# Two decoder layers' attention: the values of two jobs in a row and the scores of two more behind them, every other step

## The chip, the cores and the metric

The kernel runs on one core of one Trainium2 chip. The metric is device time in microseconds (us), of one launch from start to end. A profiled execution of the same program gives, for every instruction, its engine, start and duration. The engines are TensorE (PE for its matmuls, PEld for its weight loads), VectorE (DVE), ScalarE (ACT), GpSimd (POOL) and SyncE (SP, which issues the weights' DMAs).

## The reference, cut to what matters

The whole program is a block with a sparse-attention mixer, a cross attention and a feed-forward part, and behind it two equal layers. The change touches the attention of these two layers (16 query heads of width 64, two groups of keys and values, a band of 128 positions, so 256 keys for each block of 128 queries, and an extra sink in each softmax):

```python
def sliding_window_attention(q, k, v, sinks):      # T = 512, BLOCK = 128, 16 heads, 2 KV heads
    ...
    s = jnp.einsum('bnqkgd,bnskd->bnkgqs', qb, kb) * scale      # 128 queries x 256 keys
    s = jnp.where(mask, s, -jnp.inf)
    m = jnp.maximum(jnp.max(s, axis=-1, keepdims=True), sink)
    p = jnp.exp(s - m)
    p = p / (jnp.sum(p, axis=-1, keepdims=True) + jnp.exp(sink - m))
    o = jnp.einsum('bnkgqs,bnskd->bnqkgd', p, vb)
    ...
for l in range(2):
    ...
    a_out = sliding_window_attention(q, k, v, sinks[l])
    c_out = conformer_conv(u, ug, ...)             # 31 taps, layer norm, silu, a product
    merged = jax.nn.sigmoid(ga) * a_out + jax.nn.sigmoid(gb) * c_out
    x = x + merged @ w_out[l]
    x = x + ffn(rmsnorm(x))
```

## The kernel before

Activations lie feature-major in SBUF (128 features of a tile by 512 positions). Weights stream through three slots; each is split by ACT and DVE into a high and a low part, so a product is three matmuls of 512 columns (`products`, L415 to L417). PSUM is one tile `bank` of eight banks.

Of each layer, `layer_pe`, `layer_act`, `layer_dve` and a loop on POOL write out the order of each engine by hand. The attention of a layer is `LJ` = 32 jobs (4 query blocks by 8 pairs of heads; jobs 24 to 31 belong to the first block and have 128 keys, not 256). A loop over steps t = 0 to 35 runs through all of them, on all engines alike. In step t of the kernel before:

- PE: `scores(t)` (L2110; two heads at once on 64 rows of the array each, into banks 2 and 3 for an even job, 0 and 1 for an odd one; it waits until the softmax has read the job two before it), then `turn(t-3)` (L2120, transposes of the probabilities into bank 4; it waits for ACT's `scaled` of the job and for ACT's copy of the job turned before), then some chunks of other products (`fill_chunks`; one chunk is three matmuls of 512 columns, how many come in which step is the table `FILL_AT`), then `values(t-4)` (L2133; two heads side by side on 64 columns of the array each, into bank 6; it waits for ACT's copy of the job). In step 1 `rotate(8)` (L2028, the rotary part of the last query tile) comes between the scores and the chunks; in step 3 the sum over channels for the layer norm (L2170) is last, in step 7 its sum of squares (L333).
- ACT: `copy_turned(t-3)` (L2275, bank 4 to SBUF; it waits for PE's turn), `exps(t)` (L2260), `scaled(t-1)` (L2267, the probabilities times one over their sum), then other work of that step: tanh of a gate tile (L2293), half of a weight unit's high part (L785, L788), squares (L2299), silu (L2306) and so on.
- DVE: `softmax(t, t-1)` (L2425, mask and row maximum of job t; L2429, reciprocal of job t-1), `gated(t-4)` (L2437, the attention's result from bank 6 into the gate tile; it waits for PE's values), then evictions of finished fill tiles (L2471), halves of low parts (L793, L797), centring (L2486), taps of the convolution (L2355) in steps 0 and 1.

Every engine takes its own list strictly in this order, so whatever stands behind a waiting instruction waits as well.

Of the kernel before, what the change touches and what calls it, by code (L numbers as in the profile page):

```python
# [100 lines left out]
def build(nc, w, x, mem, pos, pack, tables, cmask, w2, wg, rope2, out):  # L101
    ctx = ExitStack()
    with ctx:
# [1742 lines left out]
        def cross_dve(dve):  # L1846
# [76 lines left out]
            for j in range(11):  # L1923
# [29 lines left out]
        FILL_FIRST = 5  # L1953
        FILL_AT = {1: 6, 2: 2, 3: 1, 5: 4, 6: 4, 7: 2, 9: 3, 10: 2, 12: 3, 14: 6, 15: 5, 16: 3, 17: 4, 18: 4, 19: 2,
                   20: 3, 21: 2, 22: 1, 23: 2, 24: 2, 25: 2, 26: 1, 27: 2, 28: 2, 29: 3, 30: 3, 31: 1}
# [11 lines left out]
        OUT_AT = {32: (0,), 33: (1,), 34: (2,), 35: (3,)}  # L1967
        STEPS = LJ + LAG_V

        def prob_at(j):  # L1970
# [27 lines left out]
        def layer_pe(pe, L):  # L1998
# [124 lines left out]
            def values(j):  # L2123
                i, g = block_of(j), j % 8 // 4
                first = 1 if i == 0 else 0
                pe.wait_ge(A["turned_copied"], L * LJ + j + 1)
                if j == 0:
                    pe.wait_ge(q_rope, L * 9 + 9)
                else:
                    pe.wait_ge(A["gated"], L * LJ + j)  # L2130
                for c in range(first, 2):
                    for e in range(2):
                        mm = pe.matmul(bank[HD * e:HD * e + HD, 6, 0:P], lv[:, i - 1 + c, g * HD:(g + 1) * HD],  # L2133
                                       lprobT[:, j % 2, 2 * e + c, :], start=(c == first), stop=(c == 1))
                mm.then_inc(A["pv"], 1)
# [11 lines left out]
            for t in range(STEPS):  # L2147
                if t < LJ:
                    scores(t)
                if t == 1:  # L2150
# [8 lines left out]
                if t in OUT_AT:  # L2159
# [3 lines left out]
                    out_products(((1, 1), (0, 0), (0, 1)), OUT_AT[t])  # L2163
                if 0 <= t - LAG_V < LJ:
                    values(t - LAG_V)
                if t == AT_SUM:
# [167 lines left out]
        def layer_dve(dve, L):  # L2334
# [96 lines left out]
            def gated(j):  # L2431
                i, tile = block_of(j), j % 8
                dst = sga[:, tile, i * P:(i + 1) * P]
                dve.wait_ge(A["pv"], L * LJ + j + 1)
                if j == 0:
                    dve.wait_ge(l_g, L * 16 + 8)
                dve.scalar_tensor_tensor(out=dst, in0=dst, scalar=1.0, in1=bank[:, 6, 0:P], op0=ALU.add, op1=ALU.mult).then_inc(A["gated"], 1)  # L2437

# [15 lines left out]
            for t in range(STEPS):  # L2454
                softmax(t, t - 1)
                if 0 <= t - LAG_V < LJ:
                    gated(t - LAG_V)
                if t == STEPS - 1:
# [292 lines left out]
```

## Time and profile before

| | us |
|---|---|
| median of 3 runs | 2248.47 |
| lowest, highest | 2247.74, 2249.46 |
| the profiled execution, its whole time | 2249.38 |
| the profiled execution, span of its instructions | 2247.4 |
| PE busy | 2225.3 (99%) |
| DVE busy | 1241.2 (55%) |
| ACT busy | 929.0 (41%) |
| POOL busy | 217.5 (10%) |

The chain of work that ended last is PE for 88% of the span, DVE for 7%, ACT for 2%. The 36 steps of the first layer lie from 1033.4 to about 1155 us of the span, those of the second from 1725.9 to about 1848. How to read it: a PE that is busy is not PE at its peak, since the ends of matmuls are modelled and overlap; the distance from the start of one group to the start of the next says more than the durations.

### The profile page before, as it was taken

To read this page: it belongs to the slowest core of one execution; us is meant where nothing else is said; L and a number is where in the kernel's file an instruction comes from. 1 tells how busy PE (TensorE), PEld (TensorE's weight loads), DVE (VectorE), ACT (ScalarE), POOL (GpSimd) and SP (SyncE) were. 2 spreads that over 40 slices of the span, in tenths; PEclk is the share of its full clock that TensorE was granted. 3 is DMA by queue.
4 is the path that set the end of the run, shared out by engine and by line. 5 is a ranking of instruction groups with operands and counts; after the bars stand their busy time and mean duration, and the time that the engine had idled before them with its cause. 6 is when DMAs were issued, how large, how long until landed. Compare 5 with 4: busy or idle time off the path is not lost.

```text
span 2247.4 us, 29309 instructions
## 1 busy us (share of the span) xinstructions
PE 2225.3 (99%) x11388; PEld 1822.5 (81%) x11388; DVE 1241.2 (55%) x1836; ACT 929.0 (41%) x1491; POOL 217.5 (10%) x209
## 2 busy tenths in 40 slices
PE   9999999999999999999999999999999999999999
PEld 7887888898888888886678888888887668888887
DVE  6467656445444225999664444333889664544422
ACT  5545454354333225235954333222323973433321
POOL 3000032011000001012031000001003122000000
PEclk9999999999999999999999999999999999999999
DMA  6221033122222231321122322222221112322222
GB/s 221 102 76 57 20 122 124 55 73 98 104 100 93 94 113 69 113 75 57 55 78 78 110 93 93 99 107 105 105 83 57 38 66 85 113 100 105 94 99 88
DMA packets 30484, 203.19 MB, mean 90 GB/s; under 512 B 3504, under 2 KB 4144, under 8 KB 6704
## 3 DMA queue, kind: packets, MB, share of 16 engines
q1 hardware_dynamic: 29088, 197.34, 24.4%
q10 hardware_dynamic: 1296, 4.46, 0.5%
q8 instruction: 69, 1.13, 0.2%
q14 instruction: 31, 0.25, 0.0%
HBM read 199.69 MB, written 2.10 MB: 90 GB/s over the span
## 4 chain that ended last, share of the span: by engine, by line
PE 88%; DVE 7%; ACT 2%; issue 2%; POOL 1%; DMA 0%; ACTq 0%; DVEq 0%; POOLq 0%
PE bank L415 25%; PE bank L417 25%; PE bank L416 25%; DVE cy L2355 3%; PE bank L2133 1%; PE bank L1002 1%; PE bank L2120 1%; PE bank L2110 1%; DVE w_lo L301 1%; PE bank L973 1%; POOL acc L324 1%; PE bank L990 1%; PE bank L2010 1%; PE bank L1593 1%; PE bank L1570 1%
## 5 line engine op out<-in xcount | busy, mean ns | idle before, releaser
L415 PE MATMUL bank<-x_hi,w_hi 128*128 128x512 f32 (+1 forms) x2032 | 790.1, 389 | 6.1 <-DVE x_lo L1766 2.3
L417 PE MATMUL bank<-x_hi,w_lo 128*128 128x512 f32 (+1 forms) x2032 | 775.0, 381 | 0.0
L416 PE MATMUL bank<-x_lo,w_hi 128*128 128x512 f32 (+1 forms) x2032 | 774.0, 381 | 0.0
L301 DVE TENSOR_TENSOR w_lo<-w_raw,w_hi 128x2048 fp32r<-128x2048 f32 x167 | 386.2, 2313 | 412.4 <-ACT w_hi L297 412.4
L297 ACT ACTIVATE w_hi<-w_raw 128x2048 fp32r<-128x2048 f32 x167 | 319.7, 1916 | 585.1 <-PE bank L417 583.2
L415 PEld LDWEIGHTS bank<-x_hi,w_hi 128*128 128x128 f32 x2032 | 382.2, 188 | 83.8 <-issue 6.8
L417 PEld LDWEIGHTS bank<-x_hi,w_lo 128*128 128x128 f32 x2032 | 381.9, 188 | 75.0
L416 PEld LDWEIGHTS bank<-x_lo,w_hi 128*128 128x128 f32 x2032 | 382.5, 188 | 72.5 <-issue 2.9
L415 PE MATMUL bank<-f_hi,w_hi 128*128 128x512 f32 (+1 forms) x572 | 213.3, 373 | 0.0
L416 PE MATMUL bank<-f_lo,w_hi 128*128 128x512 f32 (+1 forms) x572 | 213.2, 373 | 0.0
L417 PE MATMUL bank<-f_hi,w_lo 128*128 128x512 f32 (+1 forms) x572 | 213.2, 373 | 0.0
L2355 DVE SCALAR_TENSOR_TENSOR cy<-la,gains,cy 128x512 f32<-128x512 f32 x240 | 172.8, 790 | 0.0
L563 DVE TENSOR_TENSOR bank<-bank,rbc 128x512 f32<-128x512 f32 x66 | 46.0, 697 | 166.9 <-PE bank L417 158.8
L416 PEld LDWEIGHTS bank<-f_lo,w_hi 128*128 128x128 f32 x572 | 107.7, 188 | 19.1
L415 PEld LDWEIGHTS bank<-f_hi,w_hi 128*128 128x128 f32 x572 | 107.7, 188 | 18.8
L417 PEld LDWEIGHTS bank<-f_hi,w_lo 128*128 128x128 f32 x572 | 107.7, 188 | 18.8
L324 POOL TENSOR_TENSOR acc<-acc,sq 128x512 f32<-128x512 f32 (+1 forms) x48 | 77.7, 1618 | 144.2 <-ACT sq L308 140.5
L552 ACT ACTIVATE f_hi<-bank 128x512 f32 x66 | 39.6, 600 | 116.3 <-DVE bank L569 116.3
L571 DVE TENSOR_TENSOR f_lo<-bank,f_hi 128x512 f32 x66 | 45.7, 692 | 59.3 <-ACT f_hi L552 59.3
L2260 ACT ACTIVATE lprob<-lprob,small 128x257 f32<-128x257 f32 (+1 forms) x128 | 60.4, 475 | 25.4 <-DVE small L2425 25.1
L2425 DVE CUSTOM_DVE_ANT_0 lprob<-bank,mask_b,neg_sink 128x256 f32<-128x256 f32 (+1 forms) x128 | 60.0, 506 | 6.1 <-PE bank L2110 6.1
L550 ACT ACTIVATE silu<-bank 128x512 f32<-128x512 f32 x66 | 38.9, 589 | 54.7 <-DVE bank L563 54.5
(355 smaller groups left out, 2598.3 us busy)
## 6 DMA issues: line engine op xcount, KB each, us to landing
w_raw<-w_d SPq DMA_DIRECT2D x184, 1024.0 KB, 4.8
out_d<-h SPq DMA_DIRECT2D x8, 256.0 KB, 6.4
h<-x_d ACTq DMA_DIRECT2D x3, 512.0 KB, 9.4
tab<-rope_d ACTq DMA_DIRECT2D x2, 640.0 KB, 3.9
memT<-mem_d ACTq DMA_DIRECT2D x1, 1024.0 KB, 4.8
w_raw<-w_d SPq DMA_DIRECT2D x2, 256.0 KB, 4.0
h<-x_d ACTq DMA_DIRECT2D x2, 256.0 KB, 5.8
w_raw<-w_d SPq DMA_DIRECT2D x1, 512.0 KB, 6.8
```

Of the source, the lines that this page charges most:

```text
L297: act.activation(w_hi[:, u.slot, :], w_raw[:, u.slot, :], ACT.Copy).then_inc(hi_ready, 1)
L301: dve.tensor_tensor(w_lo[:, u.slot, :], w_raw[:, u.slot, :], w_hi[:, u.slot, :], ALU.subtract).then_inc(lo_ready, 1)
L324: pool.tensor_tensor(acc[:, 0:width], sq[:, 0, 0:width] if k == 1 else acc[:, 0:width], sq[:, k % 2, 0:width], ALU.add).then_inc(acc_ready, 1)
L415: pe.matmul(dst, wh[:, k, cols], hi[:, kx_, at:at + width], start=start, stop=False)
L416: pe.matmul(dst, wh[:, k, cols], lo[:, kx_, at:at + width], start=False, stop=False)
L417: return pe.matmul(dst, wl[:, k, cols], hi[:, kx_, at:at + width], start=False, stop=stop)
L552: act.activation(pick(f_hi, j, i), up, ACT.Copy).then_inc(f_hi_done, 1)
L563: dve.tensor_tensor(g, g, rbc[:, :], ALU.mult).then_inc(gu_scaled, 1)
L571: dve.tensor_tensor(pick(f_lo, j, i), up, pick(f_hi, j, i), ALU.subtract).then_inc(f_lo_done, 1)
L2260: act.activation(row, row, ACT.Exp, bias=asm(j, 0, e), scale=-1.0, accum_out=asm(j, 4, e)).then_inc(A["exp"], 1)
L2355: dve.scalar_tensor_tensor(out=cy[:, m, :], in0=src, scalar=wt, in1=cy[:, m, :], op0=ALU.mult, op1=ALU.add).then_inc(l_tap, 1)
L2425: dve.tensor_tensor_reduce(lprob[:, prob_at(j), e, c0:2 * P], bank[:, score_bank(j) + e, c0:2 * P], mask_b[:, c0:2 * P], query_factor(j, e ...
```

## The change

Two functions name the jobs of a step. `scores_at(t)`: job 0 in step 0, jobs t and t+1 in an odd step, none in an even one. `values_at(t)`: jobs t-4 and t-3 in an even step, none in an odd one. So the scores of every even job come one step earlier, and the values of every odd job one step earlier, in the very step in which it is turned. The two jobs of a pair write their values side by side in bank 6 (columns 0 to 127 and 128 to 255). DVE's `gated` of both jobs stands in the even step and waits for the values of both. One chunk moves from step 3 to step 4 and one from step 7 to step 8. Instructions, their number and their operands are otherwise the same.

```diff
-        FILL_AT = {1: 6, 2: 2, 3: 1, 5: 4, 6: 4, 7: 2, 9: 3, 10: 2, 12: 3, ...
+        FILL_AT = {1: 6, 2: 2, 4: 1, 5: 4, 6: 4, 7: 1, 8: 1, 9: 3, 10: 2, 12: 3, ...
...
+        def scores_at(t):
+            return [j for j in ((0,) if t == 0 else (t, t + 1) if t % 2 else ()) if j < LJ]
+        def values_at(t):
+            return [] if t % 2 or t < LAG_V else [t - LAG_V, t - LAG_V + 1]
...
             def values(j):
                 pe.wait_ge(A["turned_copied"], L * LJ + j + 1)
...
-                else:
+                elif j % 2 == 0:
                     pe.wait_ge(A["gated"], L * LJ + j)
...
-                        mm = pe.matmul(bank[HD * e:HD * e + HD, 6, 0:P], lv[...], lprobT[...], ...)
+                        mm = pe.matmul(bank[HD * e:HD * e + HD, 6, j % 2 * P:(j % 2 + 1) * P], lv[...], lprobT[...], ...)
...
             for t in range(STEPS):
-                if t < LJ:
-                    scores(t)
+                for j in scores_at(t):
+                    scores(j)
...
-                if 0 <= t - LAG_V < LJ:
-                    values(t - LAG_V)
+                for j in values_at(t):
+                    values(j)
...
             def gated(j):
-                dve.wait_ge(A["pv"], L * LJ + j + 1)
+                dve.wait_ge(A["pv"], L * LJ + j // 2 * 2 + 2)
...
                 softmax(t, t - 1)
-                if 0 <= t - LAG_V < LJ:
-                    gated(t - LAG_V)
+                for j in values_at(t):
+                    gated(j)
```

On PE, steps 0 and 1 of the first layer, before (L2110 scores, of jobs 0 and 1 here and of job 2 at the end; L2028 `rotate(8)`; L415 the first matmul of a chunk; 17 further rows of the six chunks are left out ahead of the last two):

```order
L2110 MATMUL bank<-lq_121 128x256
L2110 MATMUL bank<-lkx_122,lq_121 128x256
L2110 MATMUL bank<-lq_121 128x256
L2110 MATMUL bank<-lkx_122,lq_121 128x256
L2028 MATMUL bank<-lq_121,perm_q_134 128x512
L415 MATMUL bank<-x_hi_69,w_hi_65 128x512
...
L2110 MATMUL bank<-lq_121 128x256
L2110 MATMUL bank<-lkx_122,lq_121 128x256
```

The same place after (L2118 is the scores' line now, L2036 the rotation's):

```order
L2118 MATMUL bank<-lq_121 128x256
L2118 MATMUL bank<-lkx_122,lq_121 128x256
L2118 MATMUL bank<-lq_121 128x256
L2118 MATMUL bank<-lkx_122,lq_121 128x256
L2118 MATMUL bank<-lq_121 128x256
L2118 MATMUL bank<-lkx_122,lq_121 128x256
L2036 MATMUL bank<-lq_121,perm_q_134 128x512
L415 MATMUL bank<-x_hi_69,w_hi_65 128x512
```

The scores of job 2 have moved ahead of the rotation and of the six chunks of step 1.

On PE, step 4 and the start of step 5, before (scores of job 4, turn of job 1, values of job 0, scores of job 5, turn of job 2, chunks):

```order
L2110 MATMUL bank<-lkx_122,lq_121 128x256
L2110 MATMUL bank<-lq_121 128x256
L2120 MATMUL bank<-ident_50,lprob_138 128x128 x4
L2133 MATMUL bank<-lprobT_139,lv_123 64x128 x4
L2110 MATMUL bank<-lkx_122,lq_121 128x256
L2110 MATMUL bank<-lq_121 128x256
L2120 MATMUL bank<-ident_50,lprob_138 128x128 x4
L415 MATMUL bank<-x_hi_69,w_hi_65 128x512
```

The same place after (turn of job 1, a chunk, values of jobs 0 and 1, scores of jobs 5 and 6, turn of job 2):

```order
L2128 MATMUL bank<-ident_50,lprob_138 128x128 x4
L415 MATMUL bank<-x_hi_69,w_hi_65 128x512
L416 MATMUL bank<-x_lo_70,w_hi_65 128x512
L417 MATMUL bank<-x_hi_69,w_lo_66 128x512
L2141 MATMUL bank<-lprobT_139,lv_123 64x128 x8
L2118 MATMUL bank<-lkx_122,lq_121 128x256
L2118 MATMUL bank<-lq_121 128x256
L2118 MATMUL bank<-lkx_122,lq_121 128x256
L2118 MATMUL bank<-lq_121 128x256
L2128 MATMUL bank<-ident_50,lprob_138 128x128 x4
```

The values of job 1 now stand between the turn of job 1 and the scores of jobs 5 and 6, with one chunk and the values of job 0 between them and the turn; before, they stood in step 5, behind four chunks.

On DVE, the end of step 4, before (L2429 reciprocal, L2437 `gated(0)`, L793 half of a low part, L2486 centring, L2425 the softmax of step 5):

```order
L2429 RECIPROCAL small_62<-small_62 128x2
L2437 SCALAR_TENSOR_TENSOR sga_128<-sga_128,bank 128x128
L793 TENSOR_TENSOR w_lo_66<-w_raw_64,w_hi_65 128x1024
L2486 TENSOR_TENSOR cy_125<-cy_125,acc_72 128x512 x2
L2425 ISA lprob_138,small_62<-bank,mask_b_53,neg_sink_61,rcol_head_60 128x256
```

After (`gated` is L2445, of jobs 0 and 1):

```order
L2437 RECIPROCAL small_62<-small_62 128x2
L2445 SCALAR_TENSOR_TENSOR sga_128<-sga_128,bank 128x128 x2
L793 TENSOR_TENSOR w_lo_66<-w_raw_64,w_hi_65 128x1024
L2495 TENSOR_TENSOR cy_125<-cy_125,acc_72 128x512 x2
L2433 ISA lprob_138,small_62<-bank,mask_b_53,neg_sink_61,rcol_head_60 128x256
```

The split, the centring and the softmax of step 5 stand behind a `gated` that needs the values of job 1 too.

## Rows read from the trace of the kernel before

**Rows 1.** Page, busy time of the engines: share of the span, instructions.

```profile
PE 2225.3 (99%) x11388; PEld 1822.5 (81%) x11388; DVE 1241.2 (55%) x1836; ACT 929.0 (41%) x1491; POOL 217.5 (10%) x209
```

**Rows 2.** Windows: us, busy (instructions) of PE PEld DVE ACT POOL, granted clock, DMA, GB/s.

```profile
1046.00:1100.00 54.00, 52.15 (x340) 36.50 (x338) 34.61 (x110) 52.50 (x127) 8.04 (x18) 1.00 0.11 40
1100.00:1155.00 55.00, 54.38 (x354) 37.39 (x352) 35.31 (x110) 43.00 (x124) 13.56 (x18) 1.00 0.17 58
```

**Rows 3.** Timeline of PE, the turns that waited for ACT's copy: idle before in brackets.

```profile
1050.98 0.63 PE L2120 MATMUL bank<-ident,lprob 128*128 128x128 f32 x4 [1.03 <-ACT lprobT L2275]
...
1070.86 0.63 PE L2120 MATMUL bank<-ident,lprob 128*128 128x128 f32 x4 [0.82 <-ACT lprobT L2275]
```

**Rows 4.** Timeline of PE, step 11 (no chunks): start, us, line, tiles, array, form.

```profile
1073.40 0.48 PE L2110 MATMUL bank<-lq 64*128 64x256 f32 x1
1074.04 0.65 PE L2120 MATMUL bank<-ident,lprob 128*128 128x128 f32 x4
1074.62 0.66 PE L2133 MATMUL bank<-lprobT,lv 128*64 128x128 f32 x8
1075.21 0.48 PE L2110 MATMUL bank<-lkx,lq 64*128 64x256 f32 x1
```

**Rows 5.** Timeline of PE, steps 0 to 4.

```profile
1033.66 0.38 PE L2110 MATMUL bank<-lq 64*128 64x256 f32 x1
1033.88 0.38 PE L2110 MATMUL bank<-lq 64*128 64x256 f32 x1
1034.09 0.38 PE L2110 MATMUL bank<-lq 64*128 64x256 f32 x1
1034.44 1.12 PE L2028 MATMUL bank<-lq,perm_q 128*128 128x512 f32 x2
...
1039.60 0.48 PE L2110 MATMUL bank<-lq 64*128 64x256 f32 x1
1040.23 0.50 PE L415 MATMUL bank<-x_hi,w_hi 128*128 128x512 f32 x1
...
1041.81 0.48 PE L2110 MATMUL bank<-lq 64*128 64x256 f32 x1
1043.92 3.60 PE L2170 MATMUL bank<-cy,ones 128*128 128x512 f32 x8
1047.44 0.48 PE L2110 MATMUL bank<-lkx,lq 64*128 64x256 f32 x1
```

**Rows 6.** Timeline of DVE, softmax of job 0, then step 4.

```profile
1037.69 0.53 DVE L2425 CUSTOM_DVE_ANT_0 lprob<-bank,mask_b,neg_sink 128x256 f32<-128x256 f32 x1
1038.16 0.07 DVE L2425 DVE_READ_ACCUMULATOR2_ANT small<- 128x1 f32 x1
...
1050.68 1.93 DVE L793 TENSOR_TENSOR w_lo<-w_raw,w_hi 128x1024 fp32r<-128x1024 f32 x1
1052.53 1.28 DVE L2486 TENSOR_TENSOR cy<-cy,acc 128x512 f32<-128x512 f32 x2
```

**Rows 7.** Timeline of ACT, step 4 to the copy of step 5's start.

```profile
1050.26 0.58 ACT L2275 ACTIVATE lprobT<-bank 128x512 f32<-128x512 f32 x1
1050.73 0.50 ACT L2260 ACTIVATE lprob<-lprob,small 128x257 f32<-128x257 f32 x1
1051.72 0.90 ACT L2267 ACTIVATE lprob<-lprob,small 128x256 f32<-128x256 f32 x2
...
1054.51 0.58 ACT L2275 ACTIVATE lprobT<-bank 128x512 f32<-128x512 f32 x1
```

**Rows 8.** The values' line: count, duration ns min/median/max, first and last start, forms.

```profile
L2133 PE MATMUL bank<-lprobT,lv x448: 272/273/324, 1048.7 to 1847.7; 128*64 128x128 f32 x150
```

**Rows 9.** Windows, the one place where the granted clock falls.

```profile
220.88:224.29 3.41, 2.78 (x20) 2.02 (x19) 3.06 (x6) 2.57 (x7) 1.27 (x1) 1.00 0.40 171
224.29:227.70 3.41, 3.41 (x19) 3.17 (x17) 2.10 (x5) 1.27 (x4) 0.00 (x0) 0.50 0.01 2
```

**Rows 10.** Timeline of PE, just before the clock falls.

```profile
222.40 1.05 PE L333 MATMUL bank<-ones,z 128*128 128x1 f32 x8 [0.63 <-POOL z L2577]
```

More of the change, by code:

```diff
@@ L1953, in build @@
         FILL_FIRST = 5
-        FILL_AT = {1: 6, 2: 2, 3: 1, 5: 4, 6: 4, 7: 2, 9: 3, 10: 2, 12: 3, 14: 6, 15: 5, 16: 3, 17: 4, 18: 4, 19: 2,
+        FILL_AT = {1: 6, 2: 2, 4: 1, 5: 4, 6: 4, 7: 1, 8: 1, 9: 3, 10: 2, 12: 3, 14: 6, 15: 5, 16: 3, 17: 4, 18: 4, 19: 2,
                    20: 3, 21: 2, 22: 1, 23: 2, 24: 2, 25: 2, 26: 1, 27: 2, 28: 2, 29: 3, 30: 3, 31: 1}
@@ L2132, in values @@
                     for e in range(2):
-                        mm = pe.matmul(bank[HD * e:HD * e + HD, 6, 0:P], lv[:, i - 1 + c, g * HD:(g + 1) * HD],
+                        mm = pe.matmul(bank[HD * e:HD * e + HD, 6, j % 2 * P:(j % 2 + 1) * P], lv[:, i - 1 + c, g * HD:(g + 1) * HD],
                                        lprobT[:, j % 2, 2 * e + c, :], start=(c == first), stop=(c == 1))
@@ L2433, in gated @@
                 dst = sga[:, tile, i * P:(i + 1) * P]
-                dve.wait_ge(A["pv"], L * LJ + j + 1)
+                dve.wait_ge(A["pv"], L * LJ + j // 2 * 2 + 2)
                 if j == 0:
                     dve.wait_ge(l_g, L * 16 + 8)
-                dve.scalar_tensor_tensor(out=dst, in0=dst, scalar=1.0, in1=bank[:, 6, 0:P], op0=ALU.add, op1=ALU.mult).then_inc(A["gated"], 1)
+                dve.scalar_tensor_tensor(out=dst, in0=dst, scalar=1.0, in1=bank[:, 6, j % 2 * P:(j % 2 + 1) * P],
+                                         op0=ALU.add, op1=ALU.mult).then_inc(A["gated"], 1)
             def conv_gated(k):
```

## The prediction, made before the changed kernel ran

> **What bounds the kernel now.** First the page's busy line [rows 1]: PE is busy 99% of the span, ACT 41%, DVE 55%. So PE bounds the whole, and a gap or a slow stretch of PE goes into the time one for one. Then the windows of the first layer's attention [rows 2], where the shares are others: from 1046 to 1100 us (steps 3 to 16) ACT is busy 52.50 of 54 us, and from 1100 to 1155 (the rest) 43.00 of 55. In the first stretch ACT has 1.5 us of slack in all, so a faster PE can bring no more than that there, and an ACT that starts later stays late. PE's turns show the same thing: at 1050.98 and 1070.86 they had waited 1.03 and 0.82 us for ACT's copy of the job before [rows 3]. Only in the second stretch is PE alone the bound. Last, the timelines, read from start to start: they give what one group of PE's instructions costs (step 11) [rows 4], how the loop starts [rows 5], and what DVE and ACT do beside it [rows 6, 7].
>
> **What is gained: the joints.** A step without chunks is 1.81 us: scores 1073.40 to 1074.04 (0.64), turn to 1074.62 (0.58), values to 1075.21 (0.59) [rows 4]. Each of the three uses the array in another shape (64 rows, all of it, 64 columns), and part of each cost is the joint. How much, jobs in a row tell. At the start of the loop jobs 0 and 1 are scored without anything between: starts at 1033.66, 1033.88 and 1034.09, 0.215 apart, two of these to a job [rows 5]. A second job of scores thus costs 0.43, not 0.64: 0.21 saved. The eight instructions of a job's values span 0.66 us, [rows 4], of which the last takes 0.27, the line's median [rows 8], so their starts lie within 0.39, three intervals between four pairs of heads' halves, the first of them longer; a second job adds four of the short ones, about 0.11 each, 0.44 in place of 0.59: 0.15 saved. The turn of an odd step now runs into chunks or the next turn and not into values: 0.14, from the same kind of difference (0.58 for four transposes that need 0.11 each). Sum 0.50 for two steps. With 16 pairs that is 8 us a layer, 16 us in both, if PE bounded everywhere.
>
> The Trainium skill has a reason for it: "TensorEngine Tiling (Array Packing)", section Key Properties, says that a change of tiling mode, and not just of tile, drains the array. By that alone the change is a gain everywhere; its time is the first rival below.
>
> **What is lost at the start.** The scores of job 2 stand in step 1 now. Their bank is free when DVE has read job 0, and DVE does that only behind three taps: its read ends at 1038.16 + 0.07 = 1038.23 [rows 6]. PE is done with job 1 at about 1034.3 and goes on with the rotation at 1034.44 [rows 5]. In the new order it stands still from 1034.3 to 1038.3, 4 us, with rotation and six chunks queued behind. Followed on: scores of job 2 and a joint, 0.5, so the rotation starts at 1038.85, not 1034.44. Rotation and six chunks take 1039.60 - 1034.44 = 5.2, until 1044.0. Two chunks of step 2, 1.4 (1041.81 - 1040.23 is 1.58 with joints [rows 5]), then at 1045.45 two jobs of scores (1.07) and the turn of job 0 (0.45, no chunk behind it now), then the channel sum, 3.43 (1047.44 less the joint less 1043.92). It ends at 1050.4, and before it ended at 1047.35: 3.0 us late. What comes after it hangs on it: DVE's mean and centring, ACT's squares (which ended at 1050.26, when the copy of job 1 starts [rows 7]) and so that copy, now at 1053.3. That is 3.0 us on an ACT that has no slack to give back. The two edits of the table (one chunk from step 3 to 4, from 7 to 8) cost nothing by themselves: the chunk was done in step 3 ahead of the sum, and is done in step 4 ahead of the values of job 0, and no one waits for the tile that it belongs to until step 5 or 8.
>
> **What is lost in the loop.** Values of the odd job now wait for ACT's copy in the same step, and the next scores and the next turn are queued behind them. From the start of an odd job's copy to the start of the next copy PE needs: copy and signal 0.72 (1050.26 to the turn that it frees at 1050.98 [rows 3, 7]), values 0.44, joint 0.1, two jobs of scores 0.96, joint 0.1, turn 0.49, signal 0.2; 3.0 us. ACT has copy, two exponentials and two scalings to do meanwhile, 0.47 + 0.99 + 0.80 = 2.3 us [rows 7]. Before, that turn waited for the copy alone, 0.72 + 0.49 + 0.2 = 1.4, and ACT was never short of work. Where ACT is the late one and has nothing else in the step, it now idles about 0.7. In step 4 DVE adds to it: `gated` of both jobs waits for the values of job 1 (1054.0 + 0.6), and the split (1.1), the centring (1.28 for two) and the softmax of job 5 come after; so the second pair of squares ends near 1058.1 and the copy of job 2 starts there, not at 1054.51 [rows 6, 7]: 3.5 us late by then. In steps 6 to 16 I count two idle spots of 0.7 (steps 10 and 12, which have no other work on ACT) and part of a third: 5.0 us late at step 16.
>
> **What comes back.** From step 17 on PE bounds. Nine pairs at 0.50 are 4.5 us. Against it stand steps with few chunks (20, 22, 26, 28), in which the copy of the odd job is not ready when PE comes to its values; with ACT busy 43 of 55 us [rows 2], and many of its copies queued behind halves of weights, I take three waits of 0.7, 2.1 us in all. Net 2.4 back. A layer is thus 5.0 - 2.4 = 2.6 us slower, both layers 5.2.
>
> **The clock.** The new standstill of 4 us is longer than any in this trace's loops (1.03 [rows 3]). The granted clock falls once in the trace, to 0.50, the 1.2 GHz level, from 224.29 to 227.70 [rows 9]; before it PE had stood idle 0.63 us and then done eight matmuls of one column [rows 10], far less of a pause than 4 us. So I expect the fall in each layer, in or right behind the standstill. Its price by that row: it lasts 3.4 us, in which half the work is done, 1.7 us at most; part of it will lie in the standstill, where it costs nothing. Bounds 0 and 3.4 (if it takes a second such stretch to come back); I take 1.2 a layer, 2.4 in both. It delays the same chain as above, so it is added in full.
>
> The Trainium skill says so too: "TensorE: Matmul & The Clock Gate", section Why this matters for your kernels, warns that an idle gap between bursts of matmuls throws the clock back to half. Without that the sum is 5.2, with it 7.6.
>
> **The sum.** The profiled execution took 2249.38 with a span of 2247.4; it is 0.9 above the median 2248.47. The differences are the same for both: 2249.38 + 7.6 = 2257.0 for such an execution, and 2248.47 + 7.6 = 2256.0 for the median. 0.2% of it is 4.5 us, about what a measurement of this kernel can tell from no change.
>
> **The rivals.**
> - *The joints win (faster).* PE is 99% busy, and the gain of 0.50 a pair is exact arithmetic of the trace. If ACT and DVE just shift with PE and only the standstill is lost, it is 16 - 8 = 8 us less: 2240.5. Against it: ACT's 52.50 of 54 us. Chance 0.10.
> - *The standstill is swallowed (same).* PE waited 1.03 and 0.82 later anyway; if the chain behind the sum has more play than I read, what is left is the loss in the loop against what comes back, -1 to +1 a layer: 2246.5 to 2250.5, take 2249. Chance 0.14.
> - *The clock stays up.* Everything else as forecast: 2253.7. Chance 0.22.
> - *Worse.* The clock needs two stretches to come back, or the waits for copies stop PE at each of the late pairs and nothing comes back: 3 to 5 us a layer more than 2.6 to 3.8, 2261 to 2266. Chance 0.08. It decides if PE's granted clock is 0.50 for 6.8 us behind the standstill.
> - The forecast: 2256.0, with 2252.5 to 2260 as its own range. Chance 0.46.
>
> That the change doesn't do what it says is not a case: the order of PE shows the pairs at both places. The range takes the forecast, the clock that stays up and most of the swallowed standstill: 2247.5 to 2261. Slower by over 0.2%: the forecast, the worse case and two thirds of the clock case, 0.46 + 0.08 + 0.15 = 0.69, rounded to 0.70. Same: 0.07 of the clock case and nearly all of the swallowed one, 0.19. Faster 0.11.
>
> **What the profile after would show.** PE idle for 4 us ahead of the third pair of scores in each layer, released by DVE's softmax of job 0. The granted clock at 0.50 for about 3.4 us there. The channel sum of step 3 ending 3 us later against the loop's start. New waits of PE's values for ACT's copy in steps 4 and 8 and in some of the late steps, and fewer idle spots where PE's weights waited at a joint. A start to start of 0.43 for the second job of scores and 0.44 for the second of values. The forecast is wrong if ACT reaches step 16 less than 3 us late, if the late half brings more than 4 us back, or if the clock stays at 1.00.

## The result and the profile after

The changed kernel takes 2261.86 us (median of five runs, 2260.77 to 2263.60), the kernel before 2249.22 in the six runs beside it: 1.0057 of it, with an interval of 1.0047 to 1.0068, so 12.6 us slower. A sixth run of the changed kernel was in a slow state, 3156.38 us at a mean granted clock of 0.651, and with it the median is 2262.39, from which the expectations below reckon. The profiled execution took 2261.18 us with a span of 2259.2. The forecast was slower by 7.6, 2256.0, with a range to 2261: the sign came true, the size did not, and the time lies 0.9 outside the range.

The page's busy line, which answers to [rows 1]:

```profile
PE 2217.4 (98%) x11388; PEld 1826.4 (81%) x11388; DVE 1242.8 (55%) x1836; ACT 928.6 (41%) x1491; POOL 212.6 (9%) x209
```

PE is busy 7.9 us less and the span is 11.8 longer: it lost time by waiting (work at half clock counts as busy in full, so this line does not show what the clock took). The view of PE's waits (who waited for what; us in total, times, the longest) names the places. In the kernel before only the turns waited for copies, 4.8 us in all; the other lines are new:

```profile
PE bank L2141 <- ACT lprobT L2283: 10.1, 10, 1.5
PE bank L2118 <- DVE small L2433: 7.7, 2, 3.9
PE bank L2128 <- ACT lprobT L2283: 3.5, 8, 0.8
PE bank L415 <- DVE sgb L2454: 3.0, 2, 1.5
```

These are values waiting for the copy (L2141), the scores of job 2 (L2118), turns (L2128), and the first output product behind the attention (L415).

**The start.** PE's timeline, which answers to [rows 5], and the windows around it (us, then busy time and instructions of PE, PEld, DVE, ACT, POOL, the granted clock, DMA share, GB/s), which answer to [rows 9]:

```profile
1037.38 0.76 PE L2118 MATMUL bank<-lq 64*128 64x256 f32 x1 [3.87 <-DVE small L2433]
1037.94 0.63 PE L2118 MATMUL bank<-lq 64*128 64x256 f32 x1
1038.54 2.08 PE L2036 MATMUL bank<-lq,perm_q 128*128 128x512 f32 x2
```

```profile
1032.40:1035.33 2.93, 1.11 (x8) 0.71 (x8) 2.90 (x5) 0.00 (x0) 2.28 (x4) 1.00 0.00 0
1035.33:1042.16 6.83, 4.78 (x11) 2.74 (x12) 4.90 (x14) 2.99 (x10) 0.36 (x1) 0.50 0.00 0
1042.16:1046.00 3.84, 3.84 (x18) 3.18 (x17) 2.50 (x6) 0.00 (x0) 0.00 (x0) 1.00 0.00 0
...
1735.06:1741.89 6.83, 5.76 (x13) 3.52 (x14) 3.92 (x12) 2.99 (x10) 0.00 (x0) 0.50 0.00 1
```

PE stands still for 3.87 us, as forecast, and the clock falls to 1.2 GHz within that. But it stays there for 6.83 us, twice as long as in the trace before, and 4.78 of them are work at half speed. The second layer shows the same (3.88 us idle until 1736.13, clock 0.50 from 1735.06 to 1741.89), but there only 1.07 of the 6.83 us lie in the standstill, and 5.76 are work.

**The loop.** The odd job's values behind a wait for its copy, in steps 4, 8, 16 and 22, and in step 12 a turn:

```profile
1055.21 0.66 PE L2141 MATMUL bank<-lprobT,lv 128*64 128x128 f32 x8 [1.54 <-ACT lprobT L2283]
1070.75 0.66 PE L2141 MATMUL bank<-lprobT,lv 128*64 128x128 f32 x8 [1.33 <-ACT lprobT L2283]
1081.27 0.63 PE L2128 MATMUL bank<-ident,lprob 128*128 128x128 f32 x4 [0.78 <-ACT lprobT L2283]
1102.41 0.66 PE L2141 MATMUL bank<-lprobT,lv 128*64 128x128 f32 x8 [1.04 <-ACT lprobT L2283]
1123.80 0.44 PE L2141 MATMUL bank<-lprobT,lv 128*64 128x128 f32 x4 [0.78 <-ACT lprobT L2283]
```

What DVE and ACT do behind the first of them (`gated` of both jobs, the split, the centring; then ACT's copy of job 2), against [rows 6, 7]:

```profile
1055.91 0.49 DVE L2445 SCALAR_TENSOR_TENSOR sga<-sga,bank 128x128 f32<-128x128 f32 x2 [0.90 <-PE bank L2141]
1056.32 1.22 DVE L793 TENSOR_TENSOR w_lo<-w_raw,w_hi 128x1024 fp32r<-128x1024 f32 x1
1057.45 1.29 DVE L2495 TENSOR_TENSOR cy<-cy,acc 128x512 f32<-128x512 f32 x2
```

```profile
1059.31 0.58 ACT L2283 ACTIVATE lprobT<-bank 128x512 f32<-128x512 f32 x1
```

The first window of [rows 2] shows that ACT, busy 52.50 of 54 us before, now has holes, 48.96 of 54. PE sinks from 52.15 to 49.56:

```profile
1046.00:1100.00 54.00, 49.56 (x329) 36.24 (x328) 31.07 (x100) 48.96 (x119) 7.09 (x20) 1.00 0.11 40
```

That window is fixed in time, and the changed kernel reaches its work some 5 us later. From the copy of job 1 to that of job 13 ACT has the same 107 instructions in both kernels. First before, then after:

```profile
1050.26:1095.49 45.23, 43.69 (x288) 31.40 (x288) 27.98 (x88) 43.73 (x107) 7.70 (x16) 1.00 0.13 48
```

```profile
1054.58:1101.79 47.21, 43.26 (x300) 32.71 (x300) 27.05 (x88) 43.87 (x107) 6.55 (x16) 1.00 0.12 46
```

They are 43.73 and 43.87 us of work. ACT's idle time grows from 1.5 to 3.3 us, and that is nearly all of the 2.0 by which the stretch is longer.

**The joints.** Where no wait stands between, two jobs of values (1092.08) reach the next scores 1.03 us later, and two jobs of scores (1078.77) the next turn 1.06 later. Single, they took 0.59 and 0.64 [rows 4]; so the second job costs 0.44 and 0.42, and the prediction had 0.44 and 0.43.

```profile
1078.77 0.48 PE L2118 MATMUL bank<-lq 64*128 64x256 f32 x1
...
1079.83 0.66 PE L2128 MATMUL bank<-ident,lprob 128*128 128x128 f32 x4
...
1092.08 1.09 PE L2141 MATMUL bank<-lprobT,lv 128*64 128x128 f32 x16
1093.11 0.48 PE L2118 MATMUL bank<-lkx,lq 64*128 64x256 f32 x1
```

**The tail.** This part the prediction did not have. POOL's adds (L2632, the attention's result added to the convolution's) run from step 28 on, and DVE's low parts of the merged tiles (L2459) from step 30 on. DVE and POOL of the changed kernel in steps 30 and 31, and PE at its first output product of step 32:

```profile
1146.12 0.49 DVE L2445 SCALAR_TENSOR_TENSOR sga<-sga,bank 128x128 f32<-128x128 f32 x2 [0.34 <-PE bank L2141]
1146.52 1.80 DVE L2459 SCALAR_TENSOR_TENSOR o_lo<-sgb,o_hi 128x512 fp32r<-128x512 f32 x1
1148.24 0.40 DVE L2433 CUSTOM_DVE_ANT_0 lprob<-bank,mask_b,neg_sink 128x128 f32<-128x128 f32 x1
1148.98 0.66 DVE L2454 SCALAR_TENSOR_TENSOR sgb<-sgb,bank 128x512 f32<-128x512 f32 x1
```

```profile
1146.48 2.96 POOL L2632 TENSOR_TENSOR sgb<-sgb,sga 128x512 f32<-128x512 f32 x2 [3.43 <-DVE sga L2445]
```

```profile
1149.74 0.47 PE L415 MATMUL bank<-o_hi,w_hi 128*128 128x512 f32 x1 [1.48 <-DVE sgb L2454]
```

And the kernel before in step 32, where a job is gated, a low part made, and POOL's add starts (its first low part, in step 30, shows the same: 0.68 at 1141.96, with the add 0.16 behind it):

```profile
1147.16 0.29 DVE L2437 SCALAR_TENSOR_TENSOR sga<-sga,bank 128x128 f32<-128x128 f32 x1 [1.43 <-PE bank L2133]
1147.37 0.68 DVE L2450 SCALAR_TENSOR_TENSOR o_lo<-sgb,o_hi 128x512 fp32r<-128x512 f32 x1
```

```profile
1147.53 1.68 POOL L2623 TENSOR_TENSOR sgb<-sgb,sga 128x512 f32<-128x512 f32 x1 [2.42 <-DVE sga L2437]
```

Who starts first decides. Before, DVE's low part (L2450) started 0.16 us ahead of POOL's add: it took 0.68, and the add 1.68 in place of the 1.28 to 1.30 that it takes alone. Now two `gated` stand in a row, the first of them releases POOL, and POOL starts 0.04 us ahead of the low part (L2459): that takes 1.80, the last softmax and the last convolution gate (L2454) come later by it, and PE waits 1.48 us for that gate. The two seem to hold each other off, not to share: 1146.52 + 1.80 - 0.68 is 1147.64, and POOL's second add starts at 1147.73 (the row above merges the two). Of a layer's eight low parts one was stretched before, to 1.40, and four are now, to 1.78 to 1.82. The Trainium skill has this rule, in "SBUF — State Buffer", section SBUF: two separate sides: a DVE operation with two inputs in SBUF and a GpSimd one that reads SBUF compete for one pair of ports, and the first to start blocks the other for its whole length. The trace agrees, with 1.80 in place of 0.68.

The pairs also bring something here: POOL's second add comes earlier, and one half of a low part of the weights (L797, two inputs in SBUF too) is no longer beside it. Before, with POOL's add started at 1138.75, and after, with both adds ended:

```profile
1139.18 1.93 DVE L797 TENSOR_TENSOR w_lo<-w_raw,w_hi 128x1024 fp32r<-128x1024 f32 x1
```

```profile
1143.82 1.22 DVE L797 TENSOR_TENSOR w_lo<-w_raw,w_hi 128x1024 fp32r<-128x1024 f32 x1
```

**Where the time goes, by marks.** Every mark is an instruction of the first and of the second layer, in us from that layer's first scores, read from the copies' and low parts' starts and ends in each trace:

| | copy of job 1 | copy of job 13 | copy of job 28 | last low part ends |
|---|---|---|---|---|
| before | 16.89 / 16.91 | 62.12 / 62.14 | 110.06 / 110.08 | 126.42 / 126.46 |
| after | 22.20 / 22.68 | 69.41 / 69.88 | 114.98 / 115.44 | 132.56 / 133.02 |
| late by, first layer | 5.31 | 7.29 | 4.92 | 6.14 |
| late by, second layer | 5.77 | 7.74 | 5.36 | 6.56 |

So a layer loses 5.3 (5.8) at its start and 2.0 in the loop to step 16, gets 2.4 back by step 31, and loses 1.2 more in the tail. The mark of job 28 stands in a dip, though: in the first layer job 26 is still 6.56 late, job 27 5.51, job 28 4.91 and job 29 6.06 again, so the split between "back" and "tail" hangs on the mark; e9 and e10 below part the two without it. Behind the last mark nothing differs: from there to the next layer's first scores it is 566.13 before and 566.18 after. 6.14 + 6.56 = 12.7; the attention began 1.0 us earlier in this execution, for reasons ahead of the change, and 11.7 are left of the 11.8 between the spans.

### The profile page after: what moved, and what is told of

Same layout as the page of the kernel before. It is cut to its first block, busy times and chain, and to the rows that moved or that the text cites. A ratio compares the mean times of both kernels' runs of the same rounds, so it can differ in the third digit from the quotient of the medians.

```text
span 2259.2 us, 29277 instructions
## 1 busy us (share of the span) xinstructions
PE 2217.4 (98%) x11388; PEld 1826.4 (81%) x11388; DVE 1242.8 (55%) x1836; ACT 928.6 (41%) x1491; POOL 212.6 (9%) x209
## 4 chain that ended last, share of the span: by engine, by line
PE 87%; DVE 7%; ACT 3%; issue 2%; POOL 1%; DMA 0%; ACTq 0%; DVEq 0%; POOLq 0%
PE bank L415 25%; PE bank L417 25%; PE bank L416 24%; DVE cy L2363 2%; PE bank L1002 1%; PE bank L2118 1%; PE bank L2141 1%; PE bank L2128 1%; DVE w_lo L301 1%; PE bank L973 1%; POOL acc L324 1%; PE bank L2018 1%; PE bank L990 1%; PE bank L1593 1%; PE bank L1570 1%
## 5 line engine op out<-in xcount | busy, mean ns | idle before, releaser
L415 PE MATMUL bank<-x_hi,w_hi 128*128 128x512 f32 (+1 forms) x2032 | 791.9, 390 | 6.6 <-DVE w_lo L301 2.7
L415 PEld LDWEIGHTS bank<-x_hi,w_hi 128*128 128x128 f32 x2032 | 382.9, 188 | 85.0 <-issue 7.0
L415 PE MATMUL bank<-f_hi,w_hi 128*128 128x512 f32 (+1 forms) x572 | 213.3, 373 | 0.0
L415 PEld LDWEIGHTS bank<-f_hi,w_hi 128*128 128x128 f32 x572 | 107.7, 188 | 19.0
```

The source lines that it names most:

```text
L415: pe.matmul(dst, wh[:, k, cols], hi[:, kx_, at:at + width], start=start, stop=False)
```

## The experiments

Two accounts stood at the outset: that of the prediction (standstill, copies, clock), and that the pairs are a bad form as such. The ratios are each to runs of the kernel before on the same chip; "less than the changed kernel" is reckoned from its 2261.86.

**e1: no standstill.** The changed kernel with single scores at the start.

```diff
-            return [j for j in ((0,) if t == 0 else (t, t + 1) if t % 2 else ()) if j < LJ]
+            return [j for j in ((t,) if t < 5 else (t, t + 1) if t % 2 else ()) if j < LJ]
```

> The changed kernel with the scores of jobs 0 to 4 in their own steps again; pairs of scores only from jobs 5 and 6 on; the values stay in pairs. Theory A (the start: PE stands still 3.9 us for DVE's softmax of job 0, and the granted clock falls to 0.50 for 6.8 us; together the copy of job 1 starts 5.3 us late in each layer): no standstill, granted clock 1.00, the copy of job 1 in step 4 where it was before; time 2262.4 - 10.6 = 2251.8, so within 3 us of the kernel before. Theory B (the loop: values of the odd job behind ACT's copy are what costs): the time stays above 2259.

2251.70 us (2250.23 to 2253.70), ratio 1.0012 (1.0002 to 1.0022): 10.2 of the 12.6 are the start's. The copy of job 1 is at 16.90 again, that of job 13 at 64.09 (2.0 late), that of job 28 at 109.66 (0.4 early), and the last low part ends at 128.80 and 127.23. The layers differ because in the first the clock falls once, in the wait ahead of the output products:

```profile
1145.10 0.77 PE L415 MATMUL bank<-o_hi,w_hi 128*128 128x512 f32 x1 [1.48 <-DVE sgb L2454]
```

```profile
1141.60:1145.05 3.45, 1.73 (x11) 0.92 (x9) 3.45 (x10) 2.42 (x11) 2.96 (x2) 1.00 0.74 290
1145.05:1148.46 3.41, 3.36 (x8) 2.71 (x9) 0.63 (x2) 2.41 (x7) 0.00 (x0) 0.50 0.00 0
```

That stretch costs 128.80 - 127.23 = 1.6 us. The same wait of 1.48 in the changed kernel, 1149.74, brought no fall.

**e2: the standstill stays, the clock does not fall.** Seventeen matmuls of 128 columns into a free bank between the scores of jobs 1 and 2.

```diff
+                    if j == 2:
+                        for _ in range(17):
+                            pe.matmul(bank[:, 4, 0:P], ones[:, :], ones[:, :], start=True, stop=True)
                     scores(j)
```

> The changed kernel with 17 matmuls of 128 columns of ones into the free bank 4 put between the scores of jobs 1 and 2, some 3.6 us of work whose result nobody reads: PE is not idle, but is late by the same time. It parts the standstill from the clock. Theory A: the granted clock stays at 1.00, and the time falls by 2.4 us a layer (4.8 us of work that ran at half clock), to 2257.6. If the clock's price is swallowed by ACT's later lateness: 2261 to 2262.5 as before.

2258.01 us (2257.56 to 2259.31), ratio 1.0040 (1.0025 to 1.0055): 3.9 less than the changed kernel. The scores of job 2 start 5.06 us behind those of job 0, as there (1032.38 to 1037.38, 5.00), and the granted clock is 1.00 in the whole attention of both layers:

```profile
1036.52 4.06 PE L2159 MATMUL bank<-ones 128*128 128x128 f32 x34
1040.51 0.48 PE L2118 MATMUL bank<-lq 64*128 64x256 f32 x1
```

The marks of the first layer are 20.01, 67.18, 112.76 and 130.33: late by 3.12, 5.06, 2.70 and 3.91. By the marks the clock alone is thus 132.56 - 130.33 = 2.2 us in the first layer and 133.02 - 130.32 = 2.7 in the second, close to half of the 4.78 and 5.76 us of work at half speed. That is 4.9 in both, where the medians differ by 3.9; the runs of either kernel spread over 2 to 3 us.

**e3: the standstill alone.** The kernel before, with the scores of job 2 in step 1 and no other edit.

```diff
-                if t < LJ:
-                    scores(t)
+                for j in (1, 2) if t == 1 else () if t == 2 else (t,) if t < LJ else ():
+                    scores(j)
```

> The kernel before with one edit: the scores of job 2 stand in step 1, ahead of the rotation and the six chunks, and not in step 2. No pairs otherwise. Theory A: a standstill of 3.9 us in each layer, the granted clock at 0.50 for 6.8 us, the copy of job 1 about 5.3 us late, and nothing gives it back: 2249.2 + 10.6 = 2259.8. Theory B: at most 2251.

2260.82 us (2259.10 to 2261.66), ratio 1.0052 (1.0034 to 1.0070). The scores of one job in another place are nearly the whole loss, and nothing of it comes back: late by 5.78 and 4.78 at the copy of job 1, by 5.77 and 4.76 at the last low part. The 1.0 between the layers is the clock again: 6.83 us at 0.50 in the first, in the second one stretch:

```profile
1735.66:1739.07 3.41, 3.16 (x7) 1.50 (x8) 3.10 (x10) 1.58 (x7) 0.00 (x0) 0.50 0.00 0
```

**e7 and e8: one kind of pair each, without the standstill.** e7 is the kernel before with scores in pairs from step 5; e8 is the changed kernel with single scores.

```diff
-                if t < LJ:
-                    scores(t)
+                for j in [j for j in ((t,) if t < 5 else (t, t + 1) if t % 2 else ()) if j < LJ]:
+                    scores(j)
```

> The kernel before with one part alone: the scores of jobs t and t+1 together in the odd steps from 5 on, everything else as before, single values and the old chunk table included. Theory (the joint of the scores is worth 0.21 a pair, and counts only where PE bounds, from step 17 on, 7 pairs): 1.5 a layer less, 2249.9 - 3.0 = 2246.9. Rival (a pair of scores in one step asks for the softmax of the job before a step earlier, and PE waits for that what the joint saves): no difference, 2249 to 2250.5. If the joint counts everywhere: 13 pairs at 0.21, 2.7 a layer, 2244.5.

2246.98 us (2245.10 to 2249.09), ratio 0.9991 (0.9981 to 1.0001). The interval just takes in no change, but the marks are nearly the same in both layers: 0.53 late at the copy of job 13, 0.87 early at job 28, 1.06 early at the end. In the early half the pair does harm: the turn at step 10 waits longer than in [rows 3].

```profile
1070.44 0.63 PE L2120 MATMUL bank<-ident,lprob 128*128 128x128 f32 x4 [1.69 <-ACT lprobT L2275]
```

```diff
-            return [j for j in ((0,) if t == 0 else (t, t + 1) if t % 2 else ()) if j < LJ]
+            return [t] if t < LJ else []
```

> The changed kernel with the other part alone: values in pairs in the even steps, gated of both behind them, the new chunk table; scores one job a step as before, so no standstill in step 1 and the clock stays up in the attention. By the terms of the prediction: joints 0.29 a pair in 9 late pairs, 2.6 back; two idle spots of 0.7, DVE's step 4 at 0.5 and three late waits of 0.7, 4.0 lost; and the tail of 1.2 that the changed kernel shows and the prediction had not: 2.6 a layer more than before, 2255. Rival (the waits for the copies are hidden when the scores are not in pairs, since the next turn then comes a job of scores earlier): only the tail is left against the joints, -1 to +1 a layer, 2248 to 2252.

2253.14 us (2250.62 to 2255.95), ratio 1.0019 (1.0009 to 1.0028), between the two accounts. Marks of the first layer: 1.52 late at job 13, 0.23 early at job 28, 1.45 late at the end; so the tail takes 1.7, and in the second layer 3.1, with a fall of the clock in the same wait:

```profile
1839.65 0.47 PE L415 MATMUL bank<-o_hi,w_hi 128*128 128x512 f32 x1 [1.91 <-DVE sgb L2454]
```

The three late waits of values that the expectation carried over are not in it: none behind 1070 us is over 0.6. The changed kernel's waits of 1.04 and 0.78, in steps 16 and 22, need both kinds of pairs at once.

**e9 and e10: POOL's share of the tail.** The adds at 128 of 512 columns, in the changed kernel and in the one before. Three quarters of that sum are left out, so neither kernel computes the whole result; what PE, ACT and DVE do is the same.

```diff
-                    pool.tensor_tensor(sgb[:, k, :], sgb[:, k, :], sga[:, k, :], ALU.add).then_inc(mg_sum, 1)
+                    pool.tensor_tensor(sgb[:, k, 0:P], sgb[:, k, 0:P], sga[:, k, 0:P], ALU.add).then_inc(mg_sum, 1)
```

> The changed kernel, but the adds of POOL at the end of the attention (sga to sgb) take 128 of 512 columns, so three quarters of that sum are left out for 14 of the 16 tiles. Theory (two of these adds in a row, 1.3 us each, lie beside DVE's low parts and stretch them from 0.68 to 1.8 us, which makes the last softmax and the last convolution gate late and PE's first output product wait 1.48 us): each add takes about 0.35 us, the low parts 0.68, the wait of PE falls to 0.5 or less, and the time by about 1.2 a layer, to 2260. Rival (the tail is late for another reason, the pairs of values and ACT's copies): the low parts are short and the time stays at 2262 to 2262.5.

> The kernel before with the same adds of POOL at 128 of 512 columns (three quarters of that sum left out), to see whether POOL costs anything where the adds come one at a time. Both theories: PE does not wait at the output products of the kernel before, so the time stays at 2249 to 2250. If it falls too, by more than 1 us, what the narrow adds bring to the changed kernel is not its tail.

e9: 2257.53 us (2255.97 to 2258.44), ratio 1.0036 (1.0022 to 1.0050), 4.3 less than the changed kernel where 2.4 were expected. e10: 2248.75 (2247.38 to 2249.69), ratio 0.9999 (0.9989 to 1.0008). From the copy of job 1 to the last low part the narrow adds bring 110.36 - 108.69 = 1.67 us a layer in the changed kernel and 109.53 - 109.17 = 0.36 in the other; 1.3 a layer belongs to the pairs. With the adds narrow in both kernels the comeback shows without the tail: e9 against e10 is 7.25 late at the copy of job 13 and 4.79 at the last low part (6.61 and 4.18 in the second layer), 2.5 and 2.4 back. The adds and the low parts came out longer than expected (0.45 for 0.35, 0.95 to 0.98 for 0.68), and so did the wait. The low part beside a short add, and the wait that is left:

```profile
1147.88 0.96 DVE L2459 SCALAR_TENSOR_TENSOR o_lo<-sgb,o_hi 128x512 fp32r<-128x512 f32 x1
```

```profile
1147.84 1.31 POOL L2632 TENSOR_TENSOR sgb<-sgb,sga 128x128 f32<-128x128 f32 x2 [5.11 <-DVE sga L2445]
```

PE's wait at the first output product is 0.64 and 0.65, not 1.48. Of the 4.3, 3.3 is this; 1.1 is the clock, which in the profiled execution came back one stretch earlier in the second layer.

**e12: the adds whole, but one at a time.** The changed kernel with single values from job 24 on.

```diff
-            return [] if t % 2 or t < LAG_V else [t - LAG_V, t - LAG_V + 1]
+            return [t - 4] if 28 <= t else [] if t % 2 or t < LAG_V else [t - LAG_V, t - LAG_V + 1]
...
-                elif j % 2 == 0:
+                elif j % 2 == 0 or j > 24:
...
-                dve.wait_ge(A["pv"], L * LJ + j // 2 * 2 + 2)
+                dve.wait_ge(A["pv"], L * LJ + (j + 1 if j > 23 else j // 2 * 2 + 2))
```

> The changed kernel, whole, but the values (and gated) of jobs 24 to 31 one job a step as in the kernel before; the work of every engine is whole. The narrow adds brought the changed kernel 4.9 us, and showed that POOL's adds, two in a row beside DVE's low parts, are the tail. Theory (it is their coming in pairs that costs, not the adds): with single values the adds come one at a time, the low parts take 0.68, and the tail of 1.65 a layer is gone, against which four pairs lose their joints, which are worth less here (jobs of half size, 0.15 to 0.29 each, about 0.9): 0.8 a layer less, 2262.4 - 1.6 = 2260.8. Rival (the pairing of the adds is not what matters; the adds beside DVE cost the same one by one): the joints are lost and nothing comes for it, 2263 to 2264.5.

2261.23 us (2260.39 to 2262.33), ratio 1.0053 (1.0038 to 1.0068). It is 0.6 less than the changed kernel where 1.6 were expected, and by time it can't be told from it; the trace can tell. DVE is ahead of POOL again (its low part at 1153.90, POOL's add at 1154.07), and the tail from the copy of job 28 on takes 132.17 - 115.98 = 16.19 us instead of 17.58:

```profile
1153.90 0.68 DVE L2459 SCALAR_TENSOR_TENSOR o_lo<-sgb,o_hi 128x512 fp32r<-128x512 f32 x1
```

```profile
1154.07 1.68 POOL L2632 TENSOR_TENSOR sgb<-sgb,sga 128x512 f32<-128x512 f32 x1 [2.35 <-DVE sga L2445]
```

But job 28 is copied 1.0 later than in the changed kernel, while job 27 is not. Some 0.7 of that fits the same contention: POOL's add at 1145.44 lies ahead of the half of a low part (L797) at 1145.88, which takes 1.95 again and not 1.22. It is the order of the two engines that costs, not the adds; and avoiding it this way costs most of what it brings: the last low part ends 0.4 and 0.1 earlier than in the changed kernel.

**e4: the same joints without the waits.** Scores in pairs from job 6 on in even steps, values of jobs t-5 and t-4 in odd steps, so that the values never ask for a copy of their own step; for that a third buffer for the turned probabilities.

```diff
-            return [j for j in ((0,) if t == 0 else (t, t + 1) if t % 2 else ()) if j < LJ]
+            return [j for j in ((t,) if t < 6 else () if t % 2 else (t, t + 1)) if j < LJ]
...
-            return [] if t % 2 or t < LAG_V else [t - LAG_V, t - LAG_V + 1]
+            return [t - 5, t - 4] if t % 2 and t >= 5 else []
...
-                if j >= 2:
-                    act.wait_ge(A["pv"], L * LJ + j - 1)
+                if j >= 3:
+                    act.wait_ge(A["pv"], L * LJ + j - 2)
...
```

> A version that keeps both kinds of pairs but leaves the start alone and lets no value wait for a fresh copy: scores one by one up to job 5 and then jobs t and t+1 in an even step t; values of jobs t-5 and t-4 in an odd step t, so the values stand right ahead of the next step's scores and each copy is at least one step old; ACT copies into three buffers in turn, not two. By the arithmetic of the joints (0.5 us a pair) and the bound by ACT in steps 3 to 16, I expect half of 8 us a layer: 2249.2 - 8 = 2241, with no wait of the values for a copy. If ACT bounds the whole attention, or the joints are worth nothing: 2248 to 2250.

2243.32 us (2242.54 to 2244.72), ratio 0.9974 (0.9963 to 0.9985): 6.6 below the 2249.89 beside it, where 8 was expected. So the pairs are not bad as such. Marks of the first layer: as before at job 1, 0.67 early at job 13, 3.49 early at job 28, 2.76 early at the end. Between the copies of jobs 16 and 26, where PE waits for no copy longer than 0.25 us in this kernel or the one before, it gains 1.94 us (0.83 to 2.77 early), for five pairs: 0.39 a pair. At the end the tail costs here too (a low part takes 1.81, and PE waits 0.89 for a later one):

```profile
1146.12 1.81 DVE L2465 SCALAR_TENSOR_TENSOR o_lo<-sgb,o_hi 128x512 fp32r<-128x512 f32 x1
```

```profile
1154.08 0.50 PE L417 MATMUL bank<-o_hi,w_hi 128*128 128x512 f32 x1 [0.89 <-DVE o_lo L2465]
```

**e11: e4 with e12's tail.**

```diff
-            return [t - 5, t - 4] if t % 2 and t >= 5 else []
+            return [t - 4] if t > 27 else [t - 5, t - 4] if t % 2 and t >= 5 else []
...
-                elif j % 2 == 0:
+                elif j % 2 == 0 or j > 24:
...
-                dve.wait_ge(A["pv"], L * LJ + j // 2 * 2 + 2)
+                dve.wait_ge(A["pv"], L * LJ + (j + 1 if j > 23 else j // 2 * 2 + 2))
```

> The kernel with the pairs a step later (values of jobs t-5 and t-4 in odd steps, three buffers for the turned probabilities, 2243.3) with the values of jobs 24 to 31 one a step, each in step t = job + 4. In its tail the low parts took 1.03 to 1.81 us beside POOL's adds, PE waited 1.02 us at the turn of job 29 and 0.89 at the out products. Theory: both waits go or halve, 1.3 a layer, against joints of 0.9: 0.4 a layer less, 2242.5. Rival (the turn waits for ACT's copy whatever POOL does): the joints are lost, 2244 to 2245.

2242.45 us (2241.20 to 2243.20), ratio 0.9969 (0.9957 to 0.9981), the lowest of all. Against e4 the times overlap; its last low part ends at 123.13 and 122.84, 0.5 earlier in each layer. Its windows show why no more comes: in the early half ACT is the bound, as in [rows 2].

```profile
1046.00:1100.00 54.00, 50.64 (x350) 37.93 (x348) 35.02 (x109) 53.07 (x129) 8.83 (x21) 1.00 0.11 40
```

Not tried: the changed kernel with `gated` of each job in its own step and with its own wait. Both jobs' values lie in one bank, and PE would write the second while DVE reads the first, which none of these kernels does; so what DVE's longer wait in step 4 costs by itself is not parted from the 2.0 of the loop.

## Why the prediction was right or wrong

The sum was 3.0 (start) + 2.0 (loop) - 2.4 (back) + 1.2 (clock) = 3.8 a layer. Without the clock, by the marks of e2, it was 3.12 + 1.94 - 2.36 and 1.21 for the tail, 3.91; the clock took 2.2 in the first layer and 2.7 in the second: 6.1 and 6.6. Two steps failed: the clock was sized at half of what it took, and the tail was not in the sum at all.

- **The bound** (PE, with an ACT that has no slack in the first half) held. e3 shows it from the one side, 5.8 late at the start and 5.8 late at the end; e11 from the other, with ACT at 53.07 of 54.
- **The joints**: forecast 0.43 and 0.44 for a second job, measured 0.42 and 0.44. The gain is real: e4 and e11 bring it home. But the 0.50 a pair was too high: e4 gained 0.39 where PE bounds. The Trainium skill, "TensorEngine Tiling (Array Packing)", section Key Properties, states that a change of tiling mode drains TensorE; the trace agrees as far as a job with no change ahead of it is 0.15 to 0.22 cheaper. The gain everywhere that the prediction drew from it fails on what the order makes PE wait for.
- **The standstill**: forecast 4 us and the chain behind it 3.0 late; measured 3.87 and, without the clock, 3.12.
- **The loop**: forecast 2.0 more by step 16, measured 1.98 (1.94 in e2). The copies' starts show where: the lateness grows by 0.49 between the copies of jobs 1 and 2 (step 4, forecast 0.5), by 0.65 between those of jobs 7 and 8 (step 10) and by 0.50 between those of jobs 9 and 10 (step 12), forecast 0.7 each. So the places held, and the two idle spots are a little smaller. The wait of 1.33 in step 8 is among PE's longest and costs ACT nothing: job 6 is copied 0.5 less late than job 5.
- **What comes back**: forecast 2.4, measured 2.4 by the mark of job 28 (7.29 - 4.92), and 2.5 and 2.4 by e9 against e10, which need no such mark. As the difference of 4.5 from joints and three waits of 0.7 both parts were taken too high: nine pairs at e4's 0.39 are 3.5, and from step 17 on only two waits of values are over 0.3, 0.78 in step 22 and 0.35 in step 26, 1.1 in all. The two errors cancel: that the net was right is luck.
- **The clock** is the first step that failed, and as a size. I took one stretch of 3.4 us at 0.50, part of it inside the standstill, 1.2 a layer. It stayed down for 6.83 us, of which only the first 2.05 lay in the standstill (1.07 in the second layer): 4.78 and 5.76 us of work at half speed, for which e2 gives 2.2 and 2.7. The upper bound of 3.4, for two stretches, was in the prediction and holds both. This was the sign named for the worse rival, which had a chance of 0.08. It was too low: [rows 9] was one case, of a pause of 0.63 us, and says little on the length behind 4. And the length is not fixed either: e3's and e9's second layers had one stretch, for 1.0 to 1.1 us less.
- **The tail** is the step that was missing. The prediction costs what the change does to PE, ACT and DVE, and has POOL nowhere. That `gated` in pairs sends POOL's add ahead of DVE's next operation could have been asked from the order (two `gated` in a row, a low part behind them) and from the trace of before, where low part and add already touch, the one 0.68 and the other 1.68. It cost 1.2 a layer, 2.4 in all; e9 against e10 gives 1.3.

In place of 2.4 the clock took 4.9, 2.5 more, and the tail took 2.4 that stood at nothing: 7.6 and these are 12.5, against 12.6 by the times and 12.7 by the marks. With the clock alone put right the forecast would have been 2258.6, inside its range; the tail's 2.4 on top bring it to the edge, 2261.0. So the *worse* rival's range, 2261 to 2266, holds the time, but for its own reason only in part. The other rivals fell: the joints did not win (e1 shows that even without the start the kernel is 1.8 above before), the standstill was not swallowed, and the clock did fall in both layers. Of the three signs by which the forecast would be wrong none came; all three looked out for a smaller loss.

## What to carry to other kernels

Groups brought together pay when what they wait for is a step old (e4), and lose it again when one of them is put ahead of its data: the scores of a single job did nearly all the damage here (e3). A standstill of PE is paid twice, by itself and by the slow clock behind it; where the trace has only a shorter pause to go by, the forecast should take the clock's term from the upper end of its bounds. And follow the releases of an edit to the engine that seems idle: 0.2 us in the order of two starts made an operation of 0.68 us into one of 1.80.

## What the runs showed of the hardware

- Behind a standstill of 3.87 us the granted clock was 0.50 for 6.83 us in six of the eight layers that had one (after, e9, e12 and e3, with one stretch of 3.41 in the second layers of e3 and e9). In the first layer of the changed kernel it fell 1.8 us after the last matmul had ended (1033.51 to 1035.33), still inside the standstill.
- A wait of 1.48 us, with PE busy 1.73 of the 3.45 us before it, was followed by 3.41 us at 0.50 in one layer of e1, and a wait of 1.91 in one layer of e8, but the same waits in their other layers and in the changed kernel by none. Such a fall cost 1.4 to 1.6 us.
- Seventeen matmuls of 128 columns (34 records) into a bank that nobody reads then, put where PE else stood still for 3.87 us, kept the clock at 1.00 in both layers, and the time was 3.9 us lower (e2).
- A DVE operation of two SBUF inputs, 128x512, took 0.68 us alone and 1.80 when POOL's add had started 0.04 us before it; POOL's add took 1.28 to 1.30 alone and 1.68 when DVE had started first. A DVE operation of two SBUF inputs, 128x1024, took 1.22 with POOL idle and 1.93 and 1.95 when POOL's add had started 0.43 and 0.44 us before it (before, e12).
